# The scan's running-sum rows on 128 partitions instead of 16, with 112 of them zero

## The reference, cut to what matters

```python
a = (dt * A)                                   # one decay per token and head
a_cs = jnp.cumsum(a, axis=-1)                  # running sums over the tokens
diff = a_cs[..., :, None] - a_cs[..., None, :]
decay_in = where(tril, exp(where(tril, diff, 0.0)), 0.0)
cb = einsum("bclgn,bcsgn->bcgls", Cc, Bc)
y_diag = einsum("bcgls,bcgjls,bcsgjp->bclgjp", cb, decay_in, xdt)
```

## Time and profile before

| | |
|---|---|
| median of 3 runs | 3649.72 us (3649.18 to 3655.52) |
| the profiled execution's own time | 3656.93 us |
| its span, first to last instruction | 3655.2 us |
| granted PE clock, mean over the span | 0.958 |
| busy: PE, PEld, DVE, ACT, POOL | 95%, 79%, 54%, 15%, 4% |
| DMA | 153 GB/s on average |

### The profile page before, as it was taken

One profiled execution on the slowest core, in us unless ns is written; L12 is line 12 of the kernel. 1 busy time (PEld: TensorE's weight loads), 2 busy tenths in 40 slices (PEclk: granted clock), 3 DMA queues, 4 the chain that ended last, 5 costly groups with the idle time before them and its releaser, 6 DMA issues.

```text
span 3655.2 us, 54708 instructions
## 1 busy us (share of the span) xinstructions
PE 3484.4 (95%) x23626; PEld 2901.8 (79%) x23626; DVE 1966.1 (54%) x2748; ACT 548.8 (15%) x1032; POOL 161.1 (4%) x166
## 2 busy tenths in 40 slices
PE   6999999997889999999899999999999999999989
PEld 2445475545778879998799999999889968989958
DVE  3266852225556836551666666644474763385662
ACT  1000011123343421000100000000201122101130
POOL 0000002000000010000000000000050000050000
PEclk9999999998889999999999999999899979999979
DMA  8888633102323254444344444455344413344413
GB/s 341 319 333 320 266 105 125 57 12 70 89 70 80 49 188 163 169 174 156 120 172 170 163 172 166 172 185 185 123 148 152 151 69 127 128 149 158 154 45 128
DMA packets 134752, 559.43 MB, mean 153 GB/s; under 512 B 57504, under 2 KB 61856, under 8 KB 72112
## 3 DMA queue, kind: packets, MB, share of 16 engines
q1 hardware_dynamic: 120256, 456.17, 35.6%
q10 hardware_dynamic: 14304, 100.42, 6.9%
HBM read 539.24 MB, written 17.30 MB: 152 GB/s over the span
## 4 chain that ended last, share of the span: by engine, by line
PE 70%; DVE 3%; ACT 2%; SPq 1%; DMA 1%; issue 1%; DVEq 0%; ACTq 0%
PE ps L2578 14%; PE ps L465 13%; PE ps L2983 10%; PE ps L2634 7%; PE ps L2152 7%; PE ps L3527 5%; PE ps L1592 2%; PE ps L3513 1%; PE ps L1595 1%; PE ps L3399 1%; PE ps L3406 1%; PE ps L1690 1%; SPq L1413 1%; PE ps L3104 1%; DMA pack_t<-arena 0%
## 5 line engine op out<-in xcount | busy, mean ns | idle before, releaser
L465 PE MATMUL ps<-arena,ring 128*128 128x256 f32 (+3 forms) x3200 | 840.1, 425 | 27.6 <-issue 11.8
L465 PEld LDWEIGHTS ps<-arena,ring 128*128 128x128 f32 (+1 forms) x3200 | 609.4, 191 | 256.6 <-issue 183.7
L2578 PE MATMUL ps<-arena 128*128 128x128 f32 x2560 | 292.4, 275 | 0.0
L2578 PEld LDWEIGHTS ps<-arena 128*128 128x128 f32 x2560 | 289.1, 192 | 0.0
L2578 PE MATMUL ps<-arena,ring 128*128 128x128 f32 x1920 | 220.9, 275 | 0.0
L2578 PEld LDWEIGHTS ps<-arena,ring 128*128 128x128 f32 x1920 | 217.7, 192 | 0.1
L2983 PE MATMUL ps<-arena 128*128 128x128 f32 x1792 | 204.7, 275 | 0.0
L2983 PEld LDWEIGHTS ps<-arena 128*128 128x128 f32 x1792 | 202.4, 192 | 0.0
L796 DVE SCALAR_TENSOR_TENSOR arena<-arena,small 128x512 f32<-128x512 f32 x240 | 180.5, 752 | 36.6 <-DMA arena<-in_ada_late 19.9
L3527 PE MATMUL ps<-arena,ring 128*128 128x256 f32 x832 | 180.2, 379 | 0.0
L3527 PEld LDWEIGHTS ps<-arena,ring 128*128 128x128 f32 x832 | 157.9, 190 | 22.2 <-issue 1.0
(11 more groups left out here) (509 smaller groups left out, 4470.9 us busy)
## 6 DMA issues: line engine op xcount, KB each, us to landing
ring<-in_weights SPq DMA_DIRECT2D x402, 1024.0 KB, 4.8
arena<-in_ada_late ACTq DMA_DIRECT2D x64, 1024.0 KB, 8.2
arena<-in_gates SPq DMA_DIRECT2D x56, 256.0 KB, 3.4
arena<-in_front ACTq DMA_DIRECT2D x8, 1024.0 KB, 9.0
arena<-in_x ACTq DMA_DIRECT2D x2, 2048.0 KB, 12.5
keep_g<-arena SPq DMA_DIRECT2D x14, 256.0 KB, 2.0
arena<-keep_h SPq DMA_DIRECT2D x3, 1024.0 KB, 6.3
arena<-in_ctx ACTq DMA_DIRECT2D x1, 2048.0 KB, 23.8
```

The costliest lines, as they stand in the source:

```text
L465: mm = M.matmul(o, ring[:, slot, k, c0:c0 + w], rhs, start=(kc == 0), stop=(kc == ktiles * WK - 1))
L2578: mm = M.matmul(o, w[:, k], x(k), start=(k == 0), stop=(k == HD - 1))
```

## The change

`acs_rows` becomes the whole of `cos_mla`, 128 partitions. A new instruction on DVE sets it to zero once, at the head of `norm2_dve` of layer 0. ACT still writes only partitions 0 to 15, and waits once for the zeros before it does anything in `mix_act` of layer 0. `sums(h)` takes column h of the whole identity, so its product has 128 rows instead of 16, of which 112 hold zeros on the moving side; its result, 128 x 256, is the same.

```diff
-        acs_rows = C('cos_mla')[0:S_HEADS]
+        acs_rows = C('cos_mla')
...
+        rows_zero = again("rows_zero")
...
         def norm2_dve(v, l):
             if l == 0:
+                V.memset(acs_rows, 0.0).then_inc(rows_zero.sem, 1)
                 wait(v, "sq", 3)
                 square_sums(v, 1, 2)
...
         def mix_act(a, l):
+            if l == 0:
+                a.wait_ge(rows_zero.sem, 1)
...
-                                               (ACT.Copy, acs_rows, ps[0:S_HEADS, 6, T:2 * T]),
+                                               (ACT.Copy, acs_rows[0:S_HEADS], ps[0:S_HEADS, 6, T:2 * T]),
...
             def sums(h):
                 if h >= 4:
                     p.wait_ge(N['diff'].sem, N['diff'].due(p))
-                M.matmul(ps[:, h % 4, 0:T], C('ident')[0:S_HEADS, h:h + 1].to_broadcast([S_HEADS, P]), acs_rows,
+                M.matmul(ps[:, h % 4, 0:T], C('ident')[:, h:h + 1].to_broadcast([P, P]), acs_rows,
                          start=True, stop=True).then_inc(N['bc_mm'].sem, N['bc_mm'].up(p))
```

## The result

| | before | changed |
|---|---|---|
| median, us | 3650.78 (3649.18 to 3655.52, 4 runs) | 3626.81 (3624.47 to 3635.71, 4 runs) |
| ratio, 95% interval | | 0.9932 [0.9912, 0.9953] |
| profiled execution, us | 3656.93 | 3635.71 |
| its span, us | 3655.2 | 3633.9 |
| mean granted clock | 0.958 | 0.966 |

The kernel is 24.0 us or 0.66% faster by the medians; 3626 was forecast, and 24 us. The interval of the ratio goes from 17 to 32 us. The kernel before has four runs here instead of the three that the forecast started from, and a median 1.1 us higher.

A forecast was written before the change was run, and what follows sets the result against it. PE at half clock was taken to bound the two scans. 11.3 heads a layer gaining 1.05 us each gave 11.9, two layers 23.8; the median 3649.72 less that gave 3626 us, range 3618 to 3638.

The forecast's parts named there:

- The bound: In the second block's scans PE at half clock sets 2.62 us a head; DVE waits 16.2 us for it.
- The height brings the clock back: In the scans, full-height sums products return the clock from 0.50 to 1.00; products of part height leave it down.
- rival (a): The clock does not come back in the scans, as pauses or zero rows defeat it: 3650 us; chance 9%.
- When: Clock returns 4.5 us after the start of head 0, that is 1.7 heads; bounds 3.5 and 8 us.
- Does it stay: After the return PE streams 71% of a head's time at full clock, so a second fall is possible.
- rival (b): Clock comes back late, in one layer only, or falls again: half the gain, 3638 us; chance 9%.
- A head at full clock: A scan's head takes 1.57 us instead of 2.62, between 1.50 (DVE's work and starts) and 1.60 (loop through both engines).
- The sum: 11.3 of 13 heads a layer gain 1.05 us each: 11.9 a layer, 23.8 us in all, range 20 to 26.
- the last two heads and the start of the next stage: At the end of each scan, no longer at half clock until 2996; nothing was added for it.
- Rival (d): The outcome as forecast: 3626 us, own range 3619 to 3634; chance 80%.
- The zeros and the height's own price: The memset, 0.24 to 0.49 us, hides in 0.62 us of DVE idle time; taller products cost nothing visible.
- Rival (c): Slower: the full-height product in sums is dearer itself; 3687 us if each took twice its 1.15 us; chance 2%.

The follow-up runs named there:

- e2: Changed kernel with sums using 64 rows instead of 128: scans 43.8 and 43.6 us, median 3655.2 us, ratio 0.9999 to the kernel before.
- e6: Changed kernel with sums back at 16 rows and spare PE products in the idle times ahead of head 0: scans 29.1, 29.4 us, ratio 0.9934 to before.
- e1: Changed kernel without the memset and its wait, the 112 rows keeping cosines: scans 30.6 us, median 3629.7 us, ratio 0.9935 to before.
- e7: Changed kernel, sums at 128 rows, plus spare PE products in the idle times ahead of head 0: scans 29.2, 29.4 us, median 3627.1, ratio 0.9925 to before.
- e4: Changed kernel with 128 rows in sums for heads 0 to 7, 16 for heads 8 to 15: scans 30.8 us, ratio 0.9936 to before.
- e10: Changed kernel with each sums one place earlier in PE's stream: scans 28.6, 28.4 us, median 3628.1 us, ratio 0.9930 to before.
- e5: The changed kernel, unchanged, run again on another group's chip: scans 30.7, 32.2 us, median 3627.6 us, ratio 0.9927 to before.

## Why the prediction was right

**The bound.** Right. PE at half clock set 2.62 us a head; DVE's wait for sums shrank from 16.2 to 3.7 us when the clock rose.

**The height brings the clock back.** Right, and shown: with only the number of rows different, 64 (e2) leave the clock at 0.50 and 128 bring it back, and e6 shows that the clock alone is the gain. Zeros or cosines in the moving rows are the same (e1), which was half of rival (a). The forecast said nothing of how far below 128 it holds; the runs did.

**When.** Forecast 4.5 us from head 0, bounds 3.5 and 8. The two profiled scans took 4.1 and 3.7, all ten 3.3 to 6.6. The lower bound was 0.2 too high. The forecast put the fall at the beginning beside PE's 2.73 us of idle time ahead of head 0. That was misread: before, the clock fell at 2955.21 us, while the first three sums were still running and 0.1 us ahead of that idle time; the idle time that had gone before was 1.88 us, ahead of the first sums. In the changed kernel's first scan it fell 0.65 us behind the start of head 0. e6 and e7 fill both idle times, so which of the two has to be filled is open.

**Does it stay.** The second fall of rival (b) did not come: the scan, with a streaming share that the forecast put at 71%, stayed at 1.00, and e4 and e6 show that it would have with 16-row sums as well. Rival (b)'s late return is what 80 rows gave, and 96 in two scans of four.

**A head at full clock.** Forecast 1.57 between 1.50 and 1.60, measured 1.56, by the loop that was named, weigh, head, sums, diff. e10 took the loop away and reached the lower bound, DVE's own 1.50.

**The sum.** From the first sums to the last one a scan went from 37.20 us to 25.16 and 25.66, a gain of 12.0 and 11.5; forecast 11.9. From head 0 to the last sums there are 12.6 heads of 2.62 us (32.91 us) and not 13; the shorter return made up for it in part. The term that was mis-sized is the one put at nothing: the last two heads and the start of the next stage, from the last sums to the projection, went from 6.7 and 6.5 us to 5.35 in both, which is 1.3 and 1.1 a scan. The scans together gave 26.0 where 23.8 was forecast.

That the medians differ by 24.0, as forecast to a few tenths, is luck: their interval is 17 to 32 us, and on the chip of e5 the same two kernels differ by 26.4. The profiled execution took 3635.71 where 3633.1 was forecast, since it began its first scan 5.2 us later. Rival (d)'s own range of 3619 to 3634 is 1.5 us wider at each end than its terms give (3620.5 to 3632.5).

**The zeros and the height's own price.** Both nothing, as forecast (0.27 us inside 0.63 of idle time; 424 against 419 ns). Rival (c) has no ground.

## What to carry to other kernels

Look at the granted clock of each stretch before costing one: where PE is busy at 0.50 between stretches at 1.00, its work can be priced at up to twice what it need cost (here 2.62 us a head against 1.56). Products of few rows can hold the clock down though PE is hardly idle; rows of zeros, or of anything that meets zeros on the stationary side, cost no time and lifted it here. Equally good was to keep PE at work in the pause before, since a clock that is up stayed up under the same 16-row products. Judge such a change by the length of its stretch in the trace, since the total varies by more: here the first scan alone began anywhere within 19 us.

## What was not expected

- The code ahead of the first scan took 2943.8 to 2963.1 us in 13 profiled executions with almost the same instructions; by its granted clock it was at 0.50 for 184 to 239 us of them. The two hardly go together (184 us at 0.50 and a scan that began at 2950.9 in e5, 195 and 2943.8 in e2, 222 and 2947.6 in e1), so what makes the code vary stays open.
- The number of rows acts by degree: 16 and 64 of 128 did nothing, 80 gave a return after 24.9 us in both scans, 96 after 3.5, 3.6, 11.3 and 11.6, 128 after 3.3 to 6.6. Between 96 and 128 the moment of the fall is not held apart from the height.
- The demand is one-sided: 16 rows kept at 1.00, for scans of 29 us, a clock that 64 rows could not bring back in 38.
